# The expert rows of eight tokens in 16 steps, by a transfer and a step of their own

## What is computed

```python
def expert_block(args):
    xi, ii, gi = args
    u_sel = u_tab[ii]
    act = jax.nn.gelu(jnp.einsum('td,tkd->tk', xi, u_sel).astype(jnp.float32), approximate=False)
    w = (gi * act).astype(v_tab.dtype)
    return jnp.einsum('tk,tkd->td', w, v_tab[ii])
```

## Time and profile before

| | us |
|---|---|
| median of three runs | 1617.02 |
| lowest and highest run | 1616.6, 1618.84 |
| the profiled execution | 1618.45 |
| its span, first to last instruction | 1616.7 |
| busy in it: PE, DVE, ACT, POOL | 1435.8, 980.3, 667.3, 651.9 |
| its DMA engines: moved, mean rate over the span | 629.72 MB, 390 GB/s |

### The profile page before, as it was taken

The page is one execution under the profiler, slowest core; times in us unless marked ns, Lnnn a source line. Parts: engine busy times, 40 slices in busy tenths (PEclk is TensorE's granted clock), DMA queues, the critical chain, the costliest instruction groups (busy, mean ns, idle before and its releaser), DMA issues.

```text
span 1616.7 us, 14850 instructions
## 1 busy us (share of the span) xinstructions
PE 1435.8 (89%) x4450; PEld 705.7 (44%) x4450; DVE 980.3 (61%) x2487; ACT 667.3 (41%) x1841; POOL 651.9 (40%) x535
## 2 busy tenths in 40 slices
PE   7999989999867989898887999899989889797786
PEld 6646445555423434343352545355335344342222
DVE  1226578758758766743356855566456777777654
ACT  1514544544534435332243433343344454544434
POOL 1002334555434333233345334333334544556672
PEclk9999999999999999999999999999999999999999
DMA  5443999999999999999999999999999999999995
GB/s 211 156 156 134 422 419 421 421 422 421 421 422 421 421 422 421 421 422 421 421 422 421 398 422 421 422 421 415 422 422 412 422 420 422 422 421 422 421 421 217
DMA packets 87088, 629.72 MB, mean 390 GB/s; under 512 B 9808, under 2 KB 9952, under 8 KB 10720
## 3 DMA queue, kind: packets, MB, share of 16 engines
q0 software_dynamic: 73728, 536.90, 80.0%
q1 hardware_dynamic: 13104, 91.60, 13.9%
q10 hardware_dynamic: 176, 0.28, 0.1%
HBM read 627.69 MB, written 1.05 MB: 389 GB/s over the span
## 4 chain that ended last, share of the span: by engine, by line
PE 40%; DMA 38%; DVE 10%; ACT 4%; issue 4%; POOL 3%; SPq 0%; POOLq 0%; DVEq 0%; ACTq 0%
DMA ring<-in_peer_uv,experts 37%; PE acc L1569 21%; PE work L1339 6%; DVE ring L1218 5%; PE work L1356 5%; POOL ring L675 3%; PE work L1328 3%; PE acc L1532 1%; ACT diag L867 1%; PE work L1423 1%; ACT gelus L865 1%; PE work L1371 1%; DMA weights<-in_c_w_in 1%; DMA weights<-in_ab_w_in 1%; PE work L1284 1%
## 5 line engine op out<-in xcount | busy, mean ns | idle before, releaser
L1569 PE MATMUL acc<-ring,diag 128*128 128x512 f32 x2048 | 979.4, 611 | 156.9 <-ACT diag L867 155.6
L675 POOL DMA_INDIRECT ring<-in_peer_uv,experts x512 | 642.4, 1255 | 848.0 <-PE acc L1569 700.9
L1218 DVE CUSTOM_DVE_ANT_0 ring<-ring,h 128x1024 f32<-128x1024 f32 x512 | 624.2, 1227 | 431.4 <-DMA ring<-in_peer_uv,experts 423.3
L1569 PEld LDWEIGHTS acc<-ring,diag 128*128 128x128 f32 x2048 | 367.3, 191 | 687.6 <-ACT diag L867 351.1
L864 ACT ACTIVATE gelus<-dots 128x1 f32<-128x1 f32 x512 | 103.0, 201 | 677.6 <-DVE dots L1218 676.8
L867 ACT ACTIVATE diag<-ident,gelus 128x128 f32<-128x128 f32 x512 | 205.6, 402 | 16.7
L865 ACT ACTIVATE gelus<-gelus,gates 128x1 f32<-128x1 f32 x512 | 150.8, 294 | 16.6
L1339 PE MATMUL work<-weights,hT 128*128 128x512 f32 x288 | 135.0, 599 | 5.6 <-DMA weights<-in_c_w_in 5.6
L1356 PEld LDWEIGHTS work<-hT,weights 128*128 128x128 f32 x704 | 86.2, 192 | 21.0 <-issue 21.0
L1356 PE MATMUL work<-hT,weights 128*128 128x128 f32 x704 | 87.0, 275 | 0.0
L1339 PEld LDWEIGHTS work<-weights,hT 128*128 128x128 f32 x288 | 54.8, 192 | 72.2 <-issue 65.7
(11 more groups left out here) (198 smaller groups left out, 839.5 us busy)
## 6 DMA issues: line engine op xcount, KB each, us to landing
weights<-in_c_w_in SPq DMA_DIRECT2D x25, 1024.0 KB, 9.9
weights<-in_peer_w_q SPq DMA_DIRECT2D x14, 1024.0 KB, 9.6
weights<-in_ab_w_in SPq DMA_DIRECT2D x10, 1024.0 KB, 7.2
ring<-in_peer_uv,experts POOLq DMA_INDIRECT x512, 19.8
weights<-in_c_w_out SPq DMA_DIRECT2D x6, 1024.0 KB, 9.9
z<-in_c_w_out SPq DMA_DIRECT2D x6, 1024.0 KB, 11.1
z<-in_peer_w_q SPq DMA_DIRECT2D x5, 1024.0 KB, 9.2
weights<-in_ab_w_out SPq DMA_DIRECT2D x4, 1024.0 KB, 7.1
```

Source lines behind the costliest of these rows:

```text
L675: pool.indirect_dma_start(ring[:, t % SLOTS, :], None, uv_rows, bass.IndirectOffsetOnAxis(ap=experts[:, b, step:step + 1], axis=0))\
L1218: nc.vector.tensor_tensor_reduce(out=ring[:, k, 0:D], in0=ring[:, k, 0:D], in1=h[:, b, :], scale=1.0, scalar=0.0, op0=ALU.mult, op1=ALU.ad ...
L1569: last = nc.tensor.matmul(acc[2 * b + n][:, :], diag[:, k, :], ring[:, k, D + n * CH:D + (n + 1) * CH], start=False, stop=True, skip_group ...
```

## The change

The change concerns heads 2 to 5 of the last phase, and in each of them the experts k = 0, 4, 8 and 12 (`EVERY = 4`): 16 steps, each with a number j = 0 to 15 (its place in `EXTRAS`). For each of them:

- Eight tokens are set apart: the partitions 64a + 4g to 64a + 4g + 3 and those 32 higher, where a is j // 8 and g is j % 8. Over the 16 steps each token comes once, but for token 127, which is never set apart.
- The step's regular transfer gets an index out of range for these eight tokens (65,536 is added) and a bound, with the option that an index out of range is no error.
- Right behind it a second transfer into the next slot, over partitions 0 to 126 and with the same bound, has the right index for the eight tokens and one out of range for the others.
- The step's gates are zero for the eight tokens, and in the second transfer's step zero for all others. That step goes through DVE, ACT and PE like any other. The phase so has 144 steps in the ring instead of 128, and t goes on to 527.

Two tiles of 16 columns, `inside` (one for a token that column j sets apart, zero otherwise) and `lower`, are made by a new stage GROUPS on POOL behind step 4; the tile `outside` is one minus `inside`. `expert_ids` and `gate_norm` have more operations for the four heads. All new tiles lie in `stick_masks`. The change's core:

```diff
+EVERY = 4
+EXTRA_HEADS = tuple((1, 1, hd) for hd in range(2, 6))
+EXTRAS = [(layer, b, hd * TOPK + k) for layer, b, hd in EXTRA_HEADS for k in range(0, TOPK, EVERY)]
+REACH = P - 1
+FAR = 2.0 ** 16
...
+def rows_of(layer, b, i0, i1):
+
+    t = first_row(2 * layer + b) + i0 + sum((layer, b) == (l, c) and at < i0 for l, c, at in EXTRAS)
+    for step in range(i0, i1):
+        yield t, step, None
+        t += 1
+        if (layer, b, step) in EXTRAS:
+            yield t, step, EXTRAS.index((layer, b, step))
+            t += 1
...
-        + gather_with(1, 1, [(1, ("ADD", 1, 0))], parts_for(1), normed(14, "final", 0) + [(16, ("STORE", 0))])
+        + gather_with(1, 1, [(1, ("ADD", 1, 0)), (4, ("GROUPS",))], parts_for(1), normed(14, "final", 0) + [(16, ("STORE", 0))])
...
+        inside, outside, lower = (stick_masks[:, 0, i * TOPK:(i + 1) * TOPK] for i in range(3))
+        moved = stick_masks[:, 1, 0:len(EXTRAS)].bitcast(i32)
+        moved_gates = stick_masks[:, 2, 0:len(EXTRAS)]
...
+                    for tile, shift in ((inside, 0), (lower, 32)):
+                        rows = tile.rearrange("p (a g) -> p a g", a=2)
+                        linked(pool.memset(tile, 1.0))
+                        linked(pool.affine_select(out=rows, in_=rows, compare_op=ALU.is_ge, fill=0.0, base=-shift,
+                                                  pattern=[[-64, 2], [-4, 8]], channel_multiplier=1))
+                        linked(pool.affine_select(out=rows, in_=rows, compare_op=ALU.is_ge, fill=0.0, base=3 + shift,
+                                                  pattern=[[64, 2], [4, 8]], channel_multiplier=-1))
+                    linked(pool.affine_select(out=lower, in_=lower, compare_op=ALU.is_ge, fill=0.0, base=REACH - 1,
+                                              pattern=[[0, TOPK]], channel_multiplier=-1))
...
-                    for step in range(i0, i1):
-                        t = first_step(layer, b) + step
+                    for t, step, extra in rows_of(layer, b, i0, i1):
...
-                        pool.indirect_dma_start(
-                            ring[:, t % SLOTS, :], None, uv_rows,
-                            bass.IndirectOffsetOnAxis(ap=experts[:, b, step:step + 1], axis=0))\
-                            .then_inc(row_in[t % SLOTS], 16)
+                        if extra is not None:
+                            pool.indirect_dma_start(
+                                ring[0:REACH, t % SLOTS, :], None, uv_rows,
+                                bass.IndirectOffsetOnAxis(ap=moved[0:REACH, extra:extra + 1], axis=0),
+                                bounds_check=2 * NK * NK - 1, oob_is_err=False).then_inc(row_in[t % SLOTS], 16)
+                        elif (layer, b, step) in EXTRAS:
+                            pool.indirect_dma_start(
+                                ring[:, t % SLOTS, :], None, uv_rows,
+                                bass.IndirectOffsetOnAxis(ap=experts[:, b, step:step + 1], axis=0),
+                                bounds_check=2 * NK * NK - 1, oob_is_err=False).then_inc(row_in[t % SLOTS], 16)
+                        else:
+                            pool.indirect_dma_start(
+                                ring[:, t % SLOTS, :], None, uv_rows,
+                                bass.IndirectOffsetOnAxis(ap=experts[:, b, step:step + 1], axis=0))\
+                                .then_inc(row_in[t % SLOTS], 16)
...
+                        gate = gates[:, b, step:step + 1] if extra is None else moved_gates[:, extra:extra + 1]
...
+                if (layer, b, hd) in EXTRA_HEADS:
+                    j = EXTRAS.index((layer, b, hd * TOPK))
+                    own = slice(j, j + TOPK // EVERY)
+                    few = picked[:, 0, ::EVERY]
+                    dve.wait_ge(groups_made, 7)
+                    link(nc.vector.tensor_tensor(picked[:, 0, :], picked[:, 0, :], picked[:, 1, :], ALU.add))
+                    link(nc.vector.tensor_tensor(inside[:, own], inside[:, own], lower[:, own], ALU.add))
+                    link(nc.vector.tensor_scalar(outside[:, own], inside[:, own], -1.0, 1.0, ALU.mult, ALU.add))
+                    link(nc.vector.tensor_copy(head_of(experts, b, hd), picked[:, 0, :]))
+                    nc.vector.scalar_tensor_tensor(moved[:, own], outside[:, own], FAR, few, ALU.mult, ALU.add)
+                    nc.vector.scalar_tensor_tensor(head_of(experts, b, hd)[:, ::EVERY], inside[:, own], FAR, few,
+                                                   ALU.mult, ALU.add).then_inc(experts_ready, 1)
+                    return
...
+                    link(nc.vector.tensor_tensor(moved_gates[:, own], g[:, ::EVERY], inside[:, own], ALU.mult))
+                    link(nc.vector.tensor_tensor(g[:, ::EVERY], g[:, ::EVERY], outside[:, own], ALU.mult))
```

More of the change, by code:

```diff
@@ L96, with first_row @@
 TK_PARTS = 6
+EVERY = 4
[3 more added lines that the diff above has]
+FAR = 2.0 ** 16
+def first_row(phase):
+    return phase * STEPS + sum(2 * layer + b < phase for layer, b, _ in EXTRAS)
+def rows_of(layer, b, i0, i1):
[6 more added lines that the diff above has]
+            t += 1
 def gather_with(layer, b, *schedules):
@@ L1564, in _ @@
                     layer, b, i0, i1 = args
-                    for step in range(i0, i1):
-                        pe.wait_ge(diag_ready, first_step(layer, b) + step + 1)
-                        k = (first_step(layer, b) + step) % SLOTS
+                    for t, step, extra in rows_of(layer, b, i0, i1):
+                        pe.wait_ge(diag_ready, t + 1)
+                        k = t % SLOTS
                         for n in range(2):
```

28 lines of the change are left out of this document (18 added, 10 removed).

## The result

| | before | after |
|---|---|---|
| median of the runs on one chip | 1617.93 us | 1637.97 us |
| lowest to highest | 1616.6 to 1619.6 | 1636.29 to 1638.12 |
| span of the profiled execution | 1616.7 us | 1636.4 us |

The ratio is 1.012, with a 95% interval of 1.0107 to 1.0132: the change costs 20.0 us. The forecast was 1618.5 us, and its range ended at 1628. The forecast is wrong.

The account below looks back on a forecast made before the run. Expert-row transfers bound the kernel, with one late DMA engine setting the time. Completion packets 0.2, instructions 0.5 and slots 1.0 us made 1.7 us on 1617.02: 1618.7, rounded down to 1618.5 us; range 1615 to 1628.

Parts of the forecast that it names:

- The late engine sets the time: End of the trace: one DMA engine works alone for the last 11.5 us or so; the others are ahead.
- The rows themselves: Added transfers in 16 steps: same bytes; 16 completion packets each cost 0.2 us, at most 4.4 us.
- A row with an index out of range isn't moved: Both transfers of the changed steps: bytes stay the same, q0 has 73,984 packets.
- Which engine gets the rows: Added transfers: shares leave 16 engines and go to 16, sum 0; bounds from -2.5 to 37.3 us.
- The extra step's work: 16 extra steps on PE, DVE, ACT and POOL: none on the path as long as the cover lasts.
- the instructions: Some 260 more beside 14,850, about one more packet of q8: 0.5 us.
- the slots: Ring of ten: lighter slots leave 9.6 us of queue against 8.2 needed; 1 us counted for ACT's table loads.
- POOL: 16 more transfers at 1.44 us, 23 us; as a rival, POOL becomes the bound, about 1655 us, chance 0.08.
- PE's waits for diag nearly gone: Sign of being right: PE's waits, 24.2 of 150 us before, nearly vanish.
- Fetched all the same: Rival: out-of-range rows fetched, or light transfers at full cost; at least 39.8 us, 1657 or more, chance 0.03.
- Always one engine: Rival: one engine gets all added rows; 25.8 us if early, 37.3 if late, 1643 to 1654, chance 0.06.
- cover rival: Rival: queue runs empty for the late engine around steps 56 to 75; 1620.5 to 1627 us, chance 0.20.

Follow-up runs that it names:

- drop4: relief4 without its extra transfers and steps, so 32 of 65,536 rows are left out of the result; 1608.59 us against 1618.41 before.
- after128: Kernel after with the extra transfers over 128 partitions instead of 127, token 127's row moved like the others; 1620.53 us, ratio 1.0015 to before.
- near127: Kernel after with regular transfers plain and all 127 rows of each extra transfer in range, their gates zero; 1982.0 us, ratio 1.2237 to before.
- near128: Kernel after with regular transfers plain and extra transfers over 128 partitions, all rows in range, gates zero; 1659.99 us, ratio 1.0252 to before.
- relief4: Kernel after, but in only four steps the late engine's eight rows come by an extra transfer over 48 partitions; 1618.6 us, ratio 1.0001 to before.
- far124: Kernel after with regular transfers plain and extra transfers over 124 partitions, all rows out of range; 5.0 us over before.
- far64: Kernel after with regular transfers plain and extra transfers over 64 partitions, all rows out of range; 4.3 us over before.

## Why the prediction was wrong, point by point

- *The late engine sets the time*: right. drop4 showed it, with 9.8 us for 32 rows.
- *The rows themselves*: here the prediction failed, in the term for the packets. It said that each of the 16 added transfers brings 16 completion packets, 0.2 us in all and 4.4 at the most. They brought 2,048 packets each, 128 to every engine, and the partition left out alone cost 18.0 us by after128. The price was about right: 0.2 us for an engine's 16 packets is 12.5 ns each, and 9 to 10.3 were measured. The number was wrong by a factor of 128. The prediction cites that 127 partitions run on one engine, and asks only which engine would get the eight rows. It never asks how many packets the transfer makes on the fifteen others. The bound of 4.4 us rested on the count of one per engine in transfers of 128 partitions, where no row of before could show another. It bounded the price of a packet, not their number.
- *A row with an index out of range isn't moved*: right, but it isn't nothing either: it is a packet of 4 bytes. q0's bytes rose by 0.13 MB, and 64 such rows a transfer cost 4.3 us with everything else. The forecast of 73,984 packets left these out, and would have been short by 2,048 with 128 partitions too (76,032 in after128).
- *Which engine gets the rows*: near127 has one engine per transfer and not always the same, which fits the 0 of the sum. No run shows the engines of the kernel after one by one.
- *The extra step's work, the instructions, the slots*: the sum of 1.7 us stands beside 2.0 us for after128, which has all of it. One packet more of q8 came, as counted, and the transfers over the stretch land as little as 9.5 us after their issue, as forecast (some 10). That the two sums agree so well is in part luck: in after128 the DMA share does fall, to 0.85 from 1366 to 1376 us, so the cover ran out for early engines, and no term had the slower rows. Their lead took both.
- *POOL*: the bound wasn't reached, but the term was short. The added transfers took 2.85 us each and not 1.44, for 45.6 us in all instead of 23; the range test was small.
- *PE's waits for diag nearly gone*: wrong. 14.6 us remain over the same 150 us, and even in after128 8.8.
- *The rivals*: none was it. "Fetched all the same" asked for 39.8 us and more bytes in q0; near128, where the rows are in range, shows that price (41.5 us), and the kernel after doesn't pay it. "Always one engine" would have had a tail with one engine alone for 25 us and more, and it is some 4 us.
- *The range*: its upper end of 1628 came from the cover rival. A transfer shape that no row of before shows was given 0.06 + 0.03 for going badly, which was too little, and neither of the two rivals would have been the cause.

## What to carry to other kernels

Before an added indirect transfer is priced by its bytes, count its packets on every engine. In these runs each of the 16 engines got the partitions divided by k, and one packet more, where k is the largest number up to 16 that divides the partitions: 1 + 1 packets over 12 partitions, 3 + 1 over 48 (relief4: 73,984 packets in q0), 4 + 1 over 64, 8 + 1 over 128, but 31 + 1 over 124 and 127 + 1 over 127. 127 partitions instead of 128 cost 18 us over 16 transfers where almost nothing was moved, and 322 us where full rows were. Better, here, to keep the 128 partitions and mask with indices out of range, at some 10 ns a packet. If the profile after has more packets for the same bytes, look at that count first.

## What the runs showed of the hardware that I had not expected

- A transfer over 127 partitions gives all its rows to one DMA engine and 127 packets of 4 bytes to each of the fifteen others (near127: 106,496 packets in q0, 45.3 us in one wait). Over 124 partitions with nothing in range every engine gets 31 (far124: 81,920). Such a packet takes 9 ns by its record and 10.3 by the runs' times.
- POOL is busy 2.6 us or more with a transfer over 127 partitions (kernel after), 1.38 over 124 (median in far124), and 0.94 to 1.99 over 128.
- The count of bytes read from HBM takes rows out of range as read (far64: 8.39 MB for 1,024 of them), though they take no such time.
- 32 rows of 65,536 left out at the right engine gave 9.8 us, 0.6%; brought in again by another transfer, they gave nothing (relief4, 1618.60 us).
